# Matmuls without a reader at the norms of a two-layer Hyena and Mamba backbone

## The chip, the cores and the metric

The kernel runs on one core of one Trainium2 chip. The core has a matrix engine (TensorE, PE in the profile), a vector engine (VectorE, DVE), a scalar engine (ScalarE, ACT), a general engine (GpSimd, POOL) and a sync engine (SP) that issues most of the DMAs. The engines run their own instruction streams in order and meet at semaphores: an instruction can wait until a counter has reached a value, and can raise one when it is done. The metric is the device time of one execution in microseconds (us); less is better.

## The reference

Two layers over 256 latent tokens and 256 context tokens of width 1024. Every sub-layer is a norm with shift and scale, something in the middle, and a gated residual. What matters here is that each sub-layer begins with a root-mean-square over the whole width of a token, so nothing of the next product can start before the last piece of the residual stream is known:

```python
def rms_norm(x, eps=EPS):
    return x * lax.rsqrt(jnp.mean(x * x, axis=-1, keepdims=True) + eps)
def adaln(x, mod, k):
    return rms_norm(x) * (1 + mod[:, :, k + 1]) + mod[:, :, k]
def swiglu(h, w_in, w_out):
    g, u = jnp.split(h @ w_in, 2, axis=-1)
    return (jax.nn.silu(g) * u) @ w_out

h = h + 0.5 * mod[2] * swiglu(adaln(h, mod, 0), ffn_in[i, 0], ffn_out[i, 0])
a = adaln(h, mod, 3)                       # the mixer's input
y = hyena_mixer(a, ...)   # layer 0;  mamba2_mixer(a, ac, ...) in layer 1
h = h + mod[5] * y
h = h + 0.5 * mod[8] * swiglu(adaln(h, mod, 6), ffn_in[i, 1], ffn_out[i, 1])
```

The context stream does the same until the second mixer. The last line of the program is one more norm. Everything is float32.

## The kernel before, in words

The residual stream `hT` stays in SBUF as 8 tiles of 128 channels by 512 tokens (256 latent, 256 context; from the second mixer's output on only the 256 latent ones). A float32 product is done as three matmuls of a split operand pair (`mm3`, L1490): high by high, high by low, low by high. The high part of a weight chunk (`wh`, 128 x 2048) is made by ACT (`split_hi`, L553, work at L558), the low part (`wl`) by DVE (`split_lo`, L880, work at L883), both from `raw`, into which SP loads the weights. Each of the three is double-buffered. The semaphores are `w_hi`, `w_lo` (the chunk's low part is there, thus its high part too) and `w_used` (PE is done with a chunk). PSUM has eight banks of 512 columns; bank 7 belongs to the norms, and bank 0 to a chunk's first output tile.

The sub-layers have keys: "00" (FFN), "hy" (Hyena), "01" (FFN), "10" (FFN), "mb" (Mamba), "11" (FFN), "fin" (the last norm). A norm goes like this, with the engine ahead of each step:

1. DVE adds the last residual tile (L961; after the Hyena output L1193 and L1198), ACT squares it into `tt[1]` (L639), raising `sq_done`. The squares of the seven earlier tiles were added up into `acc` by POOL (L1430, `acc_done`).
2. PE sums over the channels: four matmuls with `acc` (L1502), then four with `tt[1]` (L1505), one for each 128 tokens, each one column wide (two of each for 256 tokens). The last raises `nsum`.
3. ACT takes the root (`root`, L575), DVE the reciprocal (L919, `rms_inv`).
4. PE spreads the result over the partitions with four transposes into bank 7 (L1515; two for 256 tokens), raising `rms_bc`.
5. For each of the 8 tiles k: DVE scales (`scaled`, L938), ACT makes the high part `xh` (L583), DVE the low part `xl` (`low`, L946), raising `p_lo`. DVE does them in the order scaled(0), scaled(1), low(0), scaled(2), low(1) and so on, then the low part of the second weight chunk (`second_lo`, L932). ACT makes the high part of that chunk ahead of its last tile.
6. PE starts the next sub-layer with `first_pair` (L1522): for every k it waits for `p_lo` and does the six matmuls of the first weight chunk, and then, after a wait for `w_lo` of the second chunk, the 48 matmuls of that one.

The low part of the first chunk of the next sub-layer is made before the last residual tile in four of the five norms in question ("hy", "10", "mb", "11"). In "01", which follows the Hyena output, ACT starts that split (L755) behind the last square and ahead of the root, and DVE its part (L1199) behind the last residual and ahead of the reciprocal.

The order on each engine is the order in which the code is written.

Of the kernel before, what the change touches and what calls it, by code (L numbers as in the profile page):

```python
# [11 lines left out]
P = 128  # L12
# [3 lines left out]
NT = 2 * L  # L16
# [114 lines left out]
def build(nc, t, out, kscr, afscr, cscr):  # L131
# [3 lines left out]
    ffn_in, ffn_out, norms = {}, {}, {}  # L135
# [18 lines left out]
    HYIN = Place(plan, w=12, zf=24)  # L154
# [7 lines left out]
    XB = Place(plan, w=12, conv=24)  # L162
# [8 lines left out]
    with ExitStack() as ctx:  # L171
        top = [16512]

        def at(name, shape, dt, offset):
            return nc.alloc_sbuf_tensor_at(name, shape, dt, offset=offset)
# [13 lines left out]
        def sem(name):  # L189
            return ctx.enter_context(nc.semaphore(name))  # L190
# [41 lines left out]
        wh = [at(f"wh{i}", [P, CW], F32R, o_w + i * 8 * KB) for i in range(2)]  # L232
# [55 lines left out]
        bank = [banks[i // 2][:, i % 2, :] for i in range(8)]  # L288
# [3 lines left out]
        w_lo = sem("w_lo")  # L292
# [1196 lines left out]
        def _(pe):  # L1489
            def mm3(dst, wslot, lo, x_hi, x_lo, start, stop):  # L1490

                h, l_ = wh[wslot][:, lo:lo + P], wl[wslot][:, lo:lo + P]
                pe.matmul(dst, h, x_hi, start=start, stop=False)  # L1493
                pe.matmul(dst, h, x_lo, start=False, stop=False)  # L1494
                return pe.matmul(dst, l_, x_hi, start=False, stop=stop)  # L1495

            def norm_sums(key, n=NT):
                pl = norms[key]
                cols = n // P
                pe.wait_ge(acc_done, pl.h - 1)  # L1500
                for j in range(cols):
                    pe.matmul(bank[7][:, j:j + 1], acc[:, j * P:j * P + P], ones[:, 0:1], start=j == 0, stop=False)  # L1502
                pe.wait_ge(sq_done, pl.h)
                for j in range(cols):
                    ins = pe.matmul(bank[7][:, j:j + 1], tt[1][:, j * P:j * P + P], ones[:, 0:1], start=False, stop=j == cols - 1)  # L1505
                    if j == cols - 2:
                        ins.then_inc(acc_done, 1)
                ins.then_inc(nsum, 1)

            def norm_spread(key, n=NT):  # L1510
                pl = norms[key]
                cols = n // P
                pe.wait_ge(rms_inv, pl.norm + 1)
                for j in range(cols):
                    ins = pe.transpose(bank[7][:, j * P:j * P + P], rs[:, j:j + 1].to_broadcast([P, P]), ident)  # L1515
                ins.then_inc(rms_bc, 1)

            def norm(key, n=NT):
                norm_sums(key, n)
                norm_spread(key, n)  # L1520

            def first_pair(pl, q, n=NT):  # L1522

                def tiles(u, k):
                    for s in range(2):
                        ins = mm3(bank[2 * u + s][:, 0:n], (pl.w + u) % 2, k * 256 + s * P, xh[:, k, 0:n], xl[:, k, 0:n],
                                  k == 0, k == DT - 1)
                    if k == DT - 1:
                        ins.then_inc(w_used, 1)
                pe.wait_ge(w_lo, pl.w + 1)  # L1530
                for k in range(DT):
                    pe.wait_ge(p_lo, q + k + 1)
                    tiles(0, k)
                pe.wait_ge(w_lo, pl.w + 2)
                for k in range(DT):
                    tiles(1, k)

            def two_tiles(wslot, banks, q, split=p_lo, n=NT):

                for k in range(DT):  # L1540
                    pe.wait_ge(split, q + k + 1)
                    for s in range(2):
                        ins = mm3(bank[banks + s][:, 0:n], wslot, k * 256 + s * P, xh[:, k, 0:n], xl[:, k, 0:n],
                                  k == 0, k == DT - 1)
                ins.then_inc(w_used, 1)

            def ffn(key, n=NT):

                if key != "00":
                    norm(key, n)  # L1550
                pi, po = ffn_in[key], ffn_out[key]
                x0 = norms[key].q
                def pair(i):
                    if i == 0:
                        pe.wait_ge(gate_ready, pi.gate)
                        first_pair(pi, x0, n)
                    for u in range(2 if i else 0):
                        pe.wait_ge(w_lo, i * 2 + (pi.w + u + 1))
                        if u == 0:
                            pe.wait_ge(gate_ready, i * 2 + pi.gate)  # L1560
                        else:
                            pe.wait_ge(p_ready, i * 2 + pi.q)
                        two_tiles((pi.w + u) % 2, 2 * u, x0, n=n)
                for i in range(FT // 2):
                    pair(i)

                def mpair(i, last):
                    for um in range(2):
                        pe.wait_ge(h_done, i * 2 + (po.h + um - 1))
                        for half in range(2):  # L1570
                            u = um * 2 + half
                            n_ = po.w + u
                            pe.wait_ge(w_lo, i * 4 + (n_ + 1))
                            if u == 0:
                                pe.wait_ge(p_lo, pi.q + FT - 2)
                            for kk in range(11):
                                k = half * 11 + kk
                                if k == FT - 2 and um == 0:
                                    pe.wait_ge(p_lo, pi.q + FT)
                                ins = mm3(bank[4 + um][:, 0:n], n_ % 2, kk * P, gh[:, k, 0:n], gl[:, k, 0:n],  # L1580
                                          k == 0, k == FT - 1)
                            ins.then_inc(w_used, 1)
                for i in range(DT // 2):
                    mpair(i, i == DT // 2 - 1)
# [75 lines left out]
            pe.wait_ge(mods_out, 1)  # L1660
            pe.wait_ge(s_set, 2)
            norm_sums("00")
            spectra(3, 2, 4)
            norm_spread("00")
            spectra(3, 4, 5)


            ffn("00")
            norm("hy")
            def hy_pair(i, last):  # L1670
                if i == 0:
                    pe.wait_ge(z_free, HYIN.zf)
                    first_pair(HYIN, norms["hy"].q)
                for u in range(2 if i else 0):
                    pe.wait_ge(w_lo, i * 2 + (HYIN.w + u + 1))
                    pe.wait_ge(z_free, i * 4 + (HYIN.zf + 2 * u - 2))
                    two_tiles((HYIN.w + u) % 2, 2 * u, norms["hy"].q)
# [66 lines left out]
            for j in range(4):  # L1744
# [5 lines left out]
                else:  # L1750
                    for s in range(2):
                        for k in range(DT):
                            ins = mm3(bank[2 + s][:], (HYOUT.w + 3) % 2, k * 256 + s * P, xh[:, k, :], xl[:, k, :],
                                      k == 0, k == DT - 1)
                        ins.then_inc(w_used if s else hy_half, 1)
            ffn("01")


            ffn("10")
            norm("mb")  # L1760
            x0 = norms["mb"].q

            def wide(pl, chunks, free, base, n):
# [223 lines left out]
```

## Time and profile before

| | us |
|---|---|
| three runs, median (lowest to highest) | 2147.05 (2145.24 to 2148.67) |
| the profiled execution, its own time | 2147.36 |
| its span, first to last instruction | 2145.5 |
| PE busy | 2001.8 (93%) |
| DVE busy | 1321.3 (62%) |
| ACT busy | 686.0 (32%) |
| POOL busy | 202.8 (9%) |

The mean granted TensorE clock over the span is 0.971 of full speed. In rows of the timeline the first number is the start of an instruction in us from the start of the span, the second how long it (or the run of alike instructions, "x4") took, and the bracket how long the engine had waited before it and for what.

### The profile page before, as it was taken

What the parts mean: (1) busy time and instruction counts of PE and PEld (TensorE: products, weight loads), DVE (VectorE), ACT (ScalarE), POOL (GpSimd) and SP (SyncE); (2) the same over time, 40 slices, a digit from 0 to 9 for tenths busy, and PEclk for the clock granted to TensorE, in tenths of its full rate; (3) what the DMA queues carried; (4) which work ended last, traced back from release to release, by engine and by line L of the source; (5) the groups of instructions that cost most, each with busy time, mean ns of one, the idle gap of its engine ahead of it and who ended that gap; (6) DMA issues with size and microseconds to landing.
All of it is one profiled execution on the core that took longest, in us unless ns stands there. A gap on an engine that the chain in (4) does not pass through costs nothing. (4 is left out here: it accounts for less than half of the span.)

```text
span 2145.5 us, 24954 instructions
## 1 busy us (share of the span) xinstructions
PE 2001.8 (93%) x10136; PEld 1672.0 (78%) x10136; DVE 1321.3 (62%) x1844; ACT 686.0 (32%) x913; POOL 202.8 (9%) x140
## 2 busy tenths in 40 slices
PE   5899999999989989999999999999899797698998
PEld 2688888878867868888887888888787784398998
DVE  6565546777857675554767565567765548845544
ACT  3422222232200232222224222222444335634442
POOL 1000000100023400000110000011000003340001
PEclk9999999999989999999999999999999898999999
DMA  8444435544520154442645444355432322444554
GB/s 322 152 159 155 137 106 183 165 139 135 179 76 1 41 165 148 139 155 83 201 153 171 138 152 143 104 173 165 147 118 89 118 84 74 123 133 152 186 155 141
DMA packets 274590, 298.25 MB, mean 139 GB/s; under 512 B 8912, under 2 KB 249136, under 8 KB 272688
## 3 DMA queue, kind: packets, MB, share of 16 engines
q1 hardware_dynamic: 270784, 285.44, 41.6%
q10 hardware_dynamic: 3696, 11.27, 1.4%
q8 instruction: 78, 1.28, 0.3%
q14 instruction: 32, 0.26, 0.0%
HBM read 290.31 MB, written 6.37 MB: 138 GB/s over the span
## 5 line engine op out<-in xcount | busy, mean ns | idle before, releaser
L1493 PE MATMUL banks<-xh,wh 128*128 128x512 f32 (+1 forms) x2120 | 782.3, 369 | 53.1 <-DVE xl L946 16.4
L1494 PE MATMUL banks<-xl,wh 128*128 128x512 f32 (+1 forms) x2120 | 777.0, 366 | 0.0
L1495 PE MATMUL banks<-xh,wl 128*128 128x512 f32 (+1 forms) x2120 | 776.4, 366 | 0.0
L883 DVE TENSOR_TENSOR wl<-raw,wh 128x2048 fp32r<-128x2048 f32 (+1 forms) x195 | 404.2, 2073 | 333.0 <-ACT wh L558 331.9
L558 ACT ACTIVATE wh<-raw 128x2048 fp32r<-128x2048 f32 (+1 forms) x201 | 349.6, 1739 | 644.6 <-PE banks L1495 562.9
L1493 PEld LDWEIGHTS banks<-xh,wh 128*128 128x128 f32 x2120 | 408.4, 193 | 124.5 <-issue 27.5
L1494 PEld LDWEIGHTS banks<-xl,wh 128*128 128x128 f32 x2120 | 408.4, 193 | 62.4
L1495 PEld LDWEIGHTS banks<-xh,wl 128*128 128x128 f32 x2120 | 407.8, 192 | 63.1
L1493 PE MATMUL banks<-gh,wh 128*128 128x512 f32 (+1 forms) x704 | 255.7, 363 | 2.9 <-DVE wl L883 1.6
L1494 PE MATMUL banks<-gl,wh 128*128 128x512 f32 (+1 forms) x704 | 255.2, 362 | 0.0
L1495 PE MATMUL banks<-gh,wl 128*128 128x512 f32 (+1 forms) x704 | 255.1, 362 | 0.0
L994 DVE TENSOR_TENSOR pp<-tt,banks 128x512 f32<-128x512 f32 (+1 forms) x88 | 50.7, 617 | 185.3 <-PE banks L1495 185.2
L1493 PEld LDWEIGHTS banks<-gh,wh 128*128 128x128 f32 x704 | 132.8, 189 | 24.5 <-DVE wl L883 2.2
L1494 PEld LDWEIGHTS banks<-gl,wh 128*128 128x128 f32 x704 | 132.8, 189 | 20.6
L1495 PEld LDWEIGHTS banks<-gh,wl 128*128 128x128 f32 x704 | 132.8, 189 | 20.4
L605 ACT ACTIVATE tt<-banks 128x512 f32<-128x512 f32 (+1 forms) x88 | 43.1, 542 | 271.0 <-PE banks L1495 271.0
L1430 POOL TENSOR_TENSOR acc<-acc,tt 128x512 f32<-128x512 f32 (+1 forms) x42 | 85.9, 2045 | 373.5 <-ACT tt L639 310.7
L1424 POOL MEMSET acc<- 128x512 f32 x6 | 3.2, 527 | 1176.0 <-DVE gl L974 931.4
L961 DVE SCALAR_TENSOR_TENSOR hT<-banks,mods,hT 128x256 f32<-128x256 f32 (+1 forms) x64 | 28.8, 481 | 108.2 <-PE banks L1495 108.2
L897 DVE SCALAR_TENSOR_TENSOR banks<-ada_rawo,cb 128x1024 f32<-128x1024 f32 x48 | 81.8, 1705 | 2.8 <-DMA ada_rawo<-in_ada_rest 2.8
L899 DVE SCALAR_TENSOR_TENSOR ada_rawf<-ada_rawf,cb 128x1024 f32<-128x1024 f32 x60 | 73.5, 1225 | 2.0
L897 DVE SCALAR_TENSOR_TENSOR banks<-ada_rawf,cb 128x1024 f32<-128x1024 f32 x60 | 73.7, 1228 | 0.0
(211 smaller groups left out, 1730.5 us busy)
## 6 DMA issues: line engine op xcount, KB each, us to landing
raw<-in_ffn_in SPq DMA_DIRECT2D x88, 1024.0 KB, 5.1
raw<-in_ffn_out SPq DMA_DIRECT2D x64, 704.0 KB, 4.8
ada_rawf<-in_ada_rest SPq DMA_DIRECT2D x60, 512.0 KB, 3.9
ada_rawo<-in_ada_rest SPq DMA_DIRECT2D x48, 512.0 KB, 4.0
raw<-in_mb_in_w SPq DMA_DIRECT2D x24, 1024.0 KB, 5.4
raw<-in_hy_in_w SPq DMA_DIRECT2D x12, 1024.0 KB, 5.2
afb<-decays SPq DMA_DIRECT2D x32, 256.0 KB, 3.1
raw<-in_mb_out_w SPq DMA_DIRECT2D x8, 1024.0 KB, 5.8
```

Source lines behind the costliest of these rows:

```text
L558: return act.activation(wh[n % 2][:, 0:cols], raw[r_slot][:, 0:cols], ACT.Copy).then_inc(w_hi, 1)
L605: act.activation(tt[u][:, 0:n], bank[u][:, 0:n], ACT.Silu).then_inc(gate_ready, 1)
L883: dve.tensor_tensor(wl[n_slot][:, 0:cols], raw[r_slot][:, 0:cols], wh[n_slot][:, 0:cols].bitcast(F32), ALU.subtract).then_inc(w_lo, 1)
L897: own(dve.scalar_tensor_tensor(banks[free][:].rearrange("p a n -> p (a n)"), pieces[i][:], half, cb0[:], ALU.mult, ALU.mult, accum_out=mod ...
L899: dve.scalar_tensor_tensor(pieces[i][:], pieces[i][:], half, c_ctx[:], ALU.mult, ALU.mult, accum_out=mods[layer][:, m, 1:2]).then_inc(ada_ ...
L961: ins = dve.scalar_tensor_tensor(x, bank[4 + um][:, w * L:w * L + L], mods[layer][:, i * 2 + (DT * k5 + um), w:w + 1], x, ALU.mult, ALU.add)
L994: dve.tensor_tensor(pp[(pi.q + u) % 2][:, 0:n], tt[u][:, 0:n], bank[2 + u][:, 0:n], ALU.mult).then_inc(p_ready, 1)
L1424: pool.memset(acc[:], 0.0).then_inc(acc_zero, 1)
L1430: pool.tensor_tensor(acc[:, 0:n], acc[:, 0:n], tt[um][:, 0:n], ALU.add).then_inc(acc_done, 1)
L1493: pe.matmul(dst, h, x_hi, start=start, stop=False)
L1494: pe.matmul(dst, h, x_lo, start=False, stop=False)
L1495: return pe.matmul(dst, l_, x_hi, start=False, stop=stop)
```

## The change

In five of the seven norms PE gets 19 additional matmuls, each 128 columns of `wh` of the coming chunk as the stationary operand by 512 columns of the same tile, into bank 0. Nothing reads the result: the first matmul of the next chunk begins bank 0 anew. Six stand between the sums over `acc` and the sums over the last square, two between the sums and the spread, eleven between the spread and the first chunk. Ahead of the six is a new wait for `w_lo` of the coming chunk, so that `wh` is known to be complete. The norms are "hy", "01", "10", "mb" and "11"; "00" and "fin" stay as they were. That is 5 x 19 = 95 matmuls.

```diff
+            def idle_turns(pl, count):
+                for _ in range(count):
+                    pe.matmul(bank[0][:], wh[pl.w % 2][:, 0:P], wh[pl.w % 2][:, 0:512], start=True, stop=True)
+
-            def norm_sums(key, n=NT):
+            def norm_sums(key, n=NT, nxt=None):
                 pl = norms[key]
                 cols = n // P
                 pe.wait_ge(acc_done, pl.h - 1)
                 for j in range(cols):
                     pe.matmul(bank[7][:, j:j + 1], acc[:, j * P:j * P + P], ones[:, 0:1], start=j == 0, stop=False)
+                if nxt:
+                    pe.wait_ge(w_lo, nxt.w + 1)
+                    idle_turns(nxt, 6)
                 pe.wait_ge(sq_done, pl.h)
...
-            def norm(key, n=NT):
-                norm_sums(key, n)
+            def norm(key, n=NT, nxt=None):
+                norm_sums(key, n, nxt)
+                if nxt:
+                    idle_turns(nxt, 2)
                 norm_spread(key, n)
+                if nxt:
+                    idle_turns(nxt, 11)
...
                 if key != "00":
-                    norm(key, n)
+                    norm(key, n, ffn_in[key])
...
-            norm("hy")
+            norm("hy", nxt=HYIN)
...
-            norm("mb")
+            norm("mb", nxt=XB)
```

Only PE's stream changes. At the norm "hy" it read before (`w_lo` and the other names in brackets are the semaphores waited for; `tt_114` is `tt[1]`, `wh_90` is `wh[0]`):

```order
L1502 MATMUL banks<-ones,acc 128x1 [waits acc_done]
L1502 MATMUL banks<-ones,acc 128x1 x3
L1505 MATMUL banks<-ones,tt_114 128x1 [waits sq_done]
L1505 MATMUL banks<-ones,tt_114 128x1 x3
L1515 MATMUL banks<-small,rs 128x128 [waits rms_inv]
L1515 MATMUL banks<-small,rs 128x128 x3
L1493 MATMUL banks<-xh,wh_90 128x512 [waits p_lo,w_lo,z_free]
```

and reads now (line numbers after the first added line are higher: L1506 is the old L1502, L1512 the old L1505, L1522 the old L1515, and L1499 is the added matmul):

```order
L1506 MATMUL banks<-ones,acc 128x1 [waits acc_done]
L1506 MATMUL banks<-ones,acc 128x1 x3
L1499 MATMUL banks<-wh_90 128x512 [waits w_lo]
L1499 MATMUL banks<-wh_90 128x512 x5
L1512 MATMUL banks<-ones,tt_114 128x1 [waits sq_done]
L1512 MATMUL banks<-ones,tt_114 128x1 x3
L1499 MATMUL banks<-wh_90 128x512 x2
L1522 MATMUL banks<-small,rs 128x128 [waits rms_inv]
L1522 MATMUL banks<-small,rs 128x128 x3
L1499 MATMUL banks<-wh_90 128x512 x11
L1493 MATMUL banks<-xh,wh_90 128x512 [waits p_lo,w_lo,z_free]
```

The sums over the last square now stand behind a wait for `w_lo` and six matmuls of 512 columns. At "01" and "10" the rows are the same but for `gate_ready` in place of `z_free`. At "11", the norm with 256 tokens, PE's stream was

```order
L1502 MATMUL banks<-ones,acc 128x1 [waits acc_done]
L1502 MATMUL banks<-ones,acc 128x1
L1505 MATMUL banks<-ones,tt_114 128x1 [waits sq_done]
L1505 MATMUL banks<-ones,tt_114 128x1
L1515 MATMUL banks<-small,rs 128x128 [waits rms_inv]
L1515 MATMUL banks<-small,rs 128x128
L1493 MATMUL banks<-xh,wh_91 128x256 [waits p_lo,w_lo,gate_ready]
```

and is now

```order
L1506 MATMUL banks<-ones,acc 128x1 [waits acc_done]
L1506 MATMUL banks<-ones,acc 128x1
L1499 MATMUL banks<-wh_91 128x512 [waits w_lo]
L1499 MATMUL banks<-wh_91 128x512 x5
L1512 MATMUL banks<-ones,tt_114 128x1 [waits sq_done]
L1512 MATMUL banks<-ones,tt_114 128x1
L1499 MATMUL banks<-wh_91 128x512 x2
L1522 MATMUL banks<-small,rs 128x128 [waits rms_inv]
L1522 MATMUL banks<-small,rs 128x128
L1499 MATMUL banks<-wh_91 128x512 x11
L1493 MATMUL banks<-xh,wh_91 128x256 [waits p_lo,w_lo,gate_ready]
```

The added matmuls keep their 512 columns here, while those of the sub-layer have 256.

## Rows read from the trace of the kernel before

**Rows 1.** Timeline, the norm "hy" from its sums to the first product
```profile
448.42 0.95 PE L1502 MATMUL banks<-ones,acc 128*128 128x1 f32 x8
449.53 0.63 ACT L639 ACTIVATE tt<-hT 128x512 f32<-128x512 f32 x1 [5.70 <-DVE hT L961]
450.21 1.05 PE L1505 MATMUL banks<-ones,tt 128*128 128x1 f32 x8 [0.84 <-ACT tt L639]
451.30 0.26 ACT L575 ACTIVATE rs<-banks,eps 128x4 f32<-128x4 f32 x1 [1.14 <-PE banks L1505]
...
451.83 0.75 PE L1515 MATMUL banks<-small,rs 128*128 128x128 f32 x4 [0.57 <-DVE rs L919]
452.62 1.66 DVE L938 SCALAR_TENSOR_TENSOR xt<-hT,mods,banks 128x256 f32<-128x256 f32 x4 [0.84 <-PE banks L1515]
...
455.49 0.77 PE L1493 MATMUL banks<-xh,wh 128*128 128x512 f32 x1 [2.91 <-DVE xl L946]
```

**Rows 2.** Windows, PE alone: start:end, length, busy (matmuls), PEclk, DMA share, GB/s
```profile
1000.00:1050.00 50.00, 50.00 (x223) 1.00 0.58 173
1950.00:2000.00 50.00, 50.00 (x419) 1.00 0.57 187
455.49:459.00 3.51, 3.51 (x8) 0.50 0.97 369
1939.31:1943.70 4.39, 4.39 (x20) 0.50 0.00 0
766.50:768.20 1.70, 0.00 (x0) 0.50 0.00 0
```

**Rows 3.** Timeline, the end of the first chunk of "hy" and the start of the second
```profile
466.01 0.88 DVE L946 SCALAR_TENSOR_TENSOR xl<-xt,mods,xh 128x256 fp32r<-128x256 f32 x2 [1.21 <-ACT xh L583]
466.81 2.28 DVE L932 TENSOR_TENSOR wl<-raw,wh 128x2048 fp32r<-128x2048 f32 x1
466.95 0.19 PEld L1493 LDWEIGHTS banks<-xh,wh 128*128 128x128 f32 x1 [0.38 <-DVE xl L946]
...
469.15 0.50 PE L1493 MATMUL banks<-xh,wh 128*128 128x512 f32 x1 [0.55 <-DVE wl L932]
```

**Rows 4.** Timeline, the spread of the norm "10" and what follows
```profile
1137.71 0.65 PE L1515 MATMUL banks<-small,rs 128*128 128x128 f32 x4 [0.57 <-DVE rs L919]
1138.40 1.66 DVE L938 SCALAR_TENSOR_TENSOR xt<-hT,mods,banks 128x256 f32<-128x256 f32 x4 [0.74 <-PE banks L1515]
```

**Rows 5.** Timeline, the norm "01" from the first chunk's high part to the scaling
```profile
763.95 1.89 ACT L558 ACTIVATE wh<-raw 128x2048 fp32r<-128x2048 f32 x1
764.09 1.05 PE L1505 MATMUL banks<-ones,tt 128*128 128x1 f32 x8 [1.69 <-ACT tt L639]
765.87 2.29 DVE L883 TENSOR_TENSOR wl<-raw,wh 128x2048 fp32r<-128x2048 f32 x1 [2.50 <-ACT wh L558]
768.08 0.17 DVE L919 RECIPROCAL rs<-rs 128x4 f32<-128x4 f32 x1
...
768.30 1.12 PE L1515 MATMUL banks<-small,rs 128*128 128x128 f32 x4 [3.16 <-DVE rs L919]
769.46 1.66 DVE L938 SCALAR_TENSOR_TENSOR xt<-hT,mods,banks 128x256 f32<-128x256 f32 x4 [1.21 <-PE banks L1515]
```

**Rows 6.** Timeline, the norm "11" with 256 tokens
```profile
1934.26 0.42 ACT L639 ACTIVATE tt<-hT 128x256 f32<-128x256 f32 x1 [2.45 <-DVE hT L961]
...
1934.47 1.02 PE L1502 MATMUL banks<-ones,acc 128*128 128x1 f32 x4 [3.11 <-POOL acc L1430]
...
1935.35 0.99 PE L1505 MATMUL banks<-ones,tt 128*128 128x1 f32 x4
...
1936.89 0.69 PE L1515 MATMUL banks<-small,rs 128*128 128x128 f32 x2 [0.55 <-DVE rs L919]
1937.62 0.87 DVE L938 SCALAR_TENSOR_TENSOR xt<-hT,mods,banks 128x256 f32<-128x256 f32 x2 [0.78 <-PE banks L1515]
...
1948.22 0.39 PE L1493 MATMUL banks<-xh,wh 128*128 128x256 f32 x1 [0.92 <-DVE wl L932]
```

## The prediction

> **What bounds the kernel now.** I read the page first: PE is busy 93% of the span, so what counts is the time in which it does nothing or runs at the lower clock. Then I read the granted clock in windows of 1 and 0.5 us around each norm, and the timeline of each norm. A norm is a serial chain, PE to ACT to DVE to PE to DVE, with PE mostly idle. At "hy" it goes: sums over `acc` done at 449.37, idle 0.84 until the square is there, sums from 450.21, root at 451.30, spread at 451.83, scaling at 452.62, first product at 455.49 [rows 1]. "10" and "mb" have the same pattern within 0.1 us.
>
> The clock falls to its lower level (1.2 of 2.4 GHz) in this quiet stretch: the first product of "hy" runs 8 matmuls in 3.51 us at a granted clock of 0.50, where PE at full clock does 223 in 50 us [rows 2]. That is 0.44 us against 0.224 us a matmul of 512 columns. (At half clock the steady step is 0.43: 0.427 by the starts in the timeline.) With 256 columns it is 0.22 against 50/419 = 0.119 [rows 2].
>
> Does the slow start cost anything? What the reader is to see is at the end of the first chunk. PE had caught up with DVE by the last tile: it waited 0.38 us for `xl` of the last k, and then again 0.55 us for the low part of the second chunk, which DVE started only when the last `xl` was done [rows 3]. From the scaling on, the pace is DVE's: the steps scaled and low take about 1.57 us for each k, where PE at full clock needs 6 x 0.226 = 1.36. All five norms end the first chunk with a wait of 0.5 to 0.9 us for L932; at "11" it is 0.92 [rows 6]. So in the trace the cold matmuls are hidden already, and the time at which the second chunk starts is set by `rms_bc`, that is by how soon the sums, the root and the spread are through. That short chain is what the change puts work into.
>
> **The change part by part.** An added matmul takes 0.226 us at full clock and 0.43 at half, and the first of a row some 0.11 to 0.14 more: in the timeline the second matmul behind a wait starts 0.34 (full) or 0.57 (half) after the first.
>
> *The six ahead of the last sums, "hy", "10", "mb".* They can start at about 449.30, when the sums over `acc` are issued, and take 0.11 + 6 x 0.226 = 1.47, to 450.77. The square is ready at 450.16 and its sums started at 450.21 [rows 1]. PE takes its matmuls in order, so these are late by 0.56. Bounds: 0.4 (the added row starts 0.15 sooner, under the tail of the sums) to 0.75 (the weights of the first are not loaded ahead). The spread gets a little shorter with the clock held: from its start to the scaling it is 0.79 at "hy", where the clock fell inside it, and 0.69 at "10", where it did not [rows 1, 4]; at "mb" it is 0.89. That gives back 0.1, 0 and 0.2. The wait for `w_lo` costs nothing: the low part was there at 446.2 in the timeline (L883 from 443.94, 2.29 us), ahead of the sums; without that cover it would cost as at "01". Sum of the three: 3 x 0.56 - 0.3 = 1.4; range 0.9 to 2.2.
>
> *The new wait, "01".* Here `wl` is made from 765.87 to 768.16, behind the last residual [rows 5]. Before, PE did its sums at 764.09, while ACT and DVE split the chunk, and only the reciprocal at 768.08 waited for that split. Now the sums themselves wait for it, with everything that hangs on them. PE gets through at 768.2 with the clock at 0.50 [rows 2]. Six added matmuls at half clock: 0.57 + 5 x 0.427 = 2.7, to 770.9. The sums took 0.99 for two groups of tokens at half clock [rows 6], so about 1.95 for the four of this norm, and 1.05 at full [rows 5]; root at 772.95 or 772.0. Root to spread is 0.53 [rows 1], and two cold matmuls (1.0) do not fit under it: 0.4 more. Spread to scaling takes 1.16 at half clock [rows 5], 0.69 at full [rows 4]. Scaling thus starts at 775.0 if the clock stays low, and at 773.25 if it is up by the sums, against 769.46: late by 5.5 or 3.8. I take 4.9, nearer the slow end: at "hy" the first 8 matmuls of 512 columns all ran at 0.50 [rows 2], and here only six stand ahead of the sums.
>
> *The six at "11".* `acc` is late here (PE waited 3.11 us for POOL), the clock is at 0.50, and the last square is ready at 1934.68, ahead of the end of the first sums: the second sums followed at 1935.35 without a gap [rows 6]. There is no idle time for the six to fill. They cost their full 2.7 us. The two behind the sums cost up to 0.45 if cold, nothing if the clock is up by then, and a faster spread gives back 0.2. I take 2.8; bounds 2.3 and 3.4.
>
> *The eleven behind the spread.* At full clock 0.11 + 11 x 0.226 = 2.6, against 2.9 of waiting for `xl` [rows 1]: they fit at "hy", "10", "mb". At half clock they take 4.8 and run over by 1.9 (3.1 at "11", where the wait is 1.7), but PE then does the chunk at full clock: 42 matmuls take 9.5 us, and DVE needs 466.89 - 455.35 = 11.5 to bring the last `xl`. Cost 0; bound 0.3 at "11", where 48 x 0.119 = 5.7 us of work would end just about when the second chunk is ready.
>
> *The clock in the first chunk.* The matmuls get faster, and PE waits longer for DVE instead. Gain 0; the other end is the rival below.
>
> Behind the first chunk PE is busy without a gap for tens of us [rows 2], SP's base and weight loads hang on `rms_bc` or on the splits, and all shift along. Nothing absorbs the delay.
>
> Sum: 1.4 + 4.9 + 2.8 = 9.1 us, bounds 7.0 and 11.1. The profiled execution took 2147.36, 0.3 above the median, so it stands for it: 2147.36 + 9.1 = 2156.5.
>
> **The rivals.**
>
> *The warm clock pays (the other side).* If the first chunk is paced by PE, its cold matmuls are a cost that goes away: 8, 9, 9 and 8 of 512 columns at four norms and 20 of 256 at "11", of which the first and the last are shown [rows 2], thus 34 x 0.2 + 20 x 0.1 = 8.8 us. Together with the delays 2147.7, no change; were the delays also smaller than I make them, faster, down to 2139. For it: a fall of the clock at all five norms, each with some 3.3 to 4.4 us at 0.50. Against it: the wait for the last `xl` [rows 3]. It decides from the point where PE comes to the last tile later than DVE; at "10" it was exactly level, at "11" 0.5 behind, and in both the wait for L932 was still there. The Trainium skill ("TensorE: Matmul & The Clock Gate", Why this matters for your kernels) advises to keep TensorE busy, since idle stretches between bursts send the clock to half; by it the sum would be near this rival's 2147.7. The trace agrees that the clock falls, and disagrees that here it costs.
>
> *The added matmuls make way.* If the six cost nothing at the sums, only the wait for `w_lo` at "01" is left: sums at 768.2, cold, root at 770.25, scaling at 771.95, late by 2.5: 2149.9. For it: only the idle 0.84 us at three norms. Against it: 1.47 is more than 0.84, and at "11" there is no idle time at all [rows 6]. The same page (The mechanism) has it that matmuls start and end in strict order; no row here shows a matmul that overtakes another.
>
> *The clock is not held.* The sums and the spread have columns of 1 and 128, and the clock may fall all the same. Then at "hy", "10", "mb" the two cost 0.4 and the spread is 0.4 longer, 2.4 in all, and "01" and "11" come at their slow ends, 0.6 more each: 2160.1.
>
> **How the numbers follow.** The forecast 0.72, with a range of its own of 2154.4 to 2158.5; the clock that pays 0.06; the matmuls that make way 0.10; the clock not held 0.12. About 0.2% (4.3 us) is what a measurement can tell from no change. The forecast and the third rival are slower by more: 0.84. The second rival (+2.5) and most of the first are within: 0.13. Faster is left with 0.03. The range takes in the third rival and a part of the way to the second: 2151.5 to 2160.5.
>
> **What the changed profile would show.** Right: at "hy" no idle time ahead of the sums over the square, which start 0.4 to 0.75 us after it is ready; at "01" PE idle until `wl` is done, and 6 us and more between the square and its sums; at "11" six matmuls of 0.43 us between the two rows of sums; PEclk 1.00 in the first chunks, with longer waits for `xl` in them than before, and the second chunk's start still bound to L932. From the end of the last residual to the second chunk each norm is longer by the terms above. Wrong: if that stretch is as long as before at "hy" or shorter, if PE's waits for `xl` and L932 vanish, or if the scaling at "01" begins within 3 us of where it did.

## The result and the profile after

| | before | changed |
|---|---|---|
| median of 7 runs, us (lowest to highest) | 2147.05 (2141.39 to 2148.76) | 2155.68 (2152.27 to 2158.01) |
| span of the profiled execution, us | 2145.5 | 2153.3 |
| PE busy, us | 2001.8 | 2022.3 |
| mean granted clock | 0.971 | 0.977 |

The changed kernel is slower: ratio 1.0046, 95% interval 1.0033 to 1.0059. The forecast was 2156.5. PE is busier by 20.5 us and its clock higher on the mean, and neither tells how the time changed: the 95 matmuls that nobody reads take 29.7 us of the busy time, and the first chunks, now at full clock, take less of it than before.

The norm "hy" in the timeline of the changed kernel (start, duration, engine, line; the rows answer to [rows 1]; rows of weight loads, PEld, are left out here and below):

```profile
448.73 0.94 PE L1506 MATMUL banks<-ones,acc 128*128 128x1 f32 x8
448.93 0.88 DVE L961 SCALAR_TENSOR_TENSOR hT<-banks,mods,hT 128x256 f32<-128x256 f32 x2 [2.40 <-PE banks L1495]
449.54 1.65 PE L1499 MATMUL banks<-wh 128*128 128x512 f32 x6
449.84 0.63 ACT L639 ACTIVATE tt<-hT 128x512 f32<-128x512 f32 x1 [5.71 <-DVE hT L961]
451.02 0.95 PE L1512 MATMUL banks<-ones,tt 128*128 128x1 f32 x8
451.83 0.71 PE L1499 MATMUL banks<-wh 128*128 128x512 f32 x2
452.01 0.26 ACT L575 ACTIVATE rs<-banks,eps 128x4 f32<-128x4 f32 x1 [1.53 <-PE banks L1512]
...
452.54 0.65 PE L1522 MATMUL banks<-small,rs 128*128 128x128 f32 x4
452.94 2.77 PE L1499 MATMUL banks<-wh 128*128 128x512 f32 x11
453.23 1.66 DVE L938 SCALAR_TENSOR_TENSOR xt<-hT,mods,banks 128x256 f32<-128x256 f32 x4 [0.74 <-PE banks L1522]
...
456.10 0.47 PE L1493 MATMUL banks<-xh,wh 128*128 128x512 f32 x1 [0.39 <-DVE xl L946]
```

The square is ready at 450.47, and its sums start at 451.02: the bracket with the wait for the square is gone, because PE is now the late one. Compare the bracket of 0.84 before [rows 1]. From the start of these sums to the scaling it is 2.21 us instead of 2.41. Half of the 0.20 is the spread, 0.65 us instead of 0.75, with the clock held. The other half is the sums, 0.95 instead of 1.05, and this is not the clock, which was full in both: they now follow other matmuls without idle time. Net 0.30 later. The first product waits 0.39 for `xl` instead of 2.91, which sounds like a gain and is none: the eleven only fill the time.

The end of the first chunk (to be laid beside [rows 3]):

```profile
466.62 0.88 DVE L946 SCALAR_TENSOR_TENSOR xl<-xt,mods,xh 128x256 fp32r<-128x256 f32 x2 [1.21 <-ACT xh L583]
467.42 2.28 DVE L932 TENSOR_TENSOR wl<-raw,wh 128x2048 fp32r<-128x2048 f32 x1
467.56 0.50 PE L1493 MATMUL banks<-xh,wh 128*128 128x512 f32 x1 [0.42 <-DVE xl L946]
...
469.76 0.50 PE L1493 MATMUL banks<-xh,wh 128*128 128x512 f32 x1 [0.55 <-DVE wl L932]
```

From the scaling (453.23) to the second chunk (469.76) it is 16.53 us. Before it was 469.15 - 452.62 = 16.53.

The norm "01" (beside [rows 5]):

```profile
761.27 0.69 DVE L1198 TENSOR_TENSOR hT<-hT,tt 128x512 f32<-128x512 f32 x1
761.99 0.63 ACT L639 ACTIVATE tt<-hT 128x512 f32<-128x512 f32 x1 [4.80 <-DVE hT L1198]
762.53 1.89 ACT L558 ACTIVATE wh<-raw 128x2048 fp32r<-128x2048 f32 x1
764.45 2.29 DVE L883 TENSOR_TENSOR wl<-raw,wh 128x2048 fp32r<-128x2048 f32 x1 [2.50 <-ACT wh L558]
766.80 2.93 PE L1499 MATMUL banks<-wh 128*128 128x512 f32 x6 [5.82 <-DVE wl L883]
769.53 1.70 PE L1512 MATMUL banks<-ones,tt 128*128 128x1 f32 x8
771.09 1.20 PE L1499 MATMUL banks<-wh 128*128 128x512 f32 x2
...
772.09 1.05 PE L1522 MATMUL banks<-small,rs 128*128 128x128 f32 x4
772.79 3.82 PE L1499 MATMUL banks<-wh 128*128 128x512 f32 x11
773.18 1.65 DVE L938 SCALAR_TENSOR_TENSOR xt<-hT,mods,banks 128x256 f32<-128x256 f32 x4 [1.44 <-PE banks L1522]
```

The new wait shows as a bracket of 5.82 us for L883 where 1.69 for the square stood. The sums start 6.91 us after the square is ready, not 0.05. The six run at half clock, and so do the sums (1.70) and the spread (1.05): the granted clock over each of the three is 0.50.

The norm "11" (beside [rows 6]):

```profile
1938.40 0.61 PE L1506 MATMUL banks<-ones,acc 128*128 128x1 f32 x4 [3.09 <-POOL acc L1430]
1938.87 2.81 PE L1499 MATMUL banks<-wh 128*128 128x512 f32 x6
1941.47 0.85 PE L1512 MATMUL banks<-ones,tt 128*128 128x1 f32 x4
...
1942.87 0.43 PE L1522 MATMUL banks<-small,rs 128*128 128x128 f32 x2
1943.06 2.75 PE L1499 MATMUL banks<-wh 128*128 128x512 f32 x11
1943.34 0.87 DVE L938 SCALAR_TENSOR_TENSOR xt<-hT,mods,banks 128x256 f32<-128x256 f32 x2 [0.53 <-PE banks L1522]
```

The square (ready at 1938.61) waits 2.86 us for PE. The six (2.60 from start to start) and the last sums ran at a granted clock of 0.50, the sums over `acc` and the spread at full clock.

Divided at the start of the scaling, the five norms give the account. "Ahead" is from the end of the last residual tile (L961, at "01" L1198) to the first L938, "behind" from there to the first matmul of the second chunk, both read from row starts:

| norm | ahead, before | ahead, changed | behind, before | behind, changed | forecast | measured |
|---|---|---|---|---|---|---|
| hy | 3.12 | 3.42 | 16.53 | 16.53 | +0.46 | +0.30 |
| 01 | 6.09 | 11.22 | 16.53 | 16.53 | +4.9 | +5.13 |
| 10 | 3.02 | 3.42 | 16.53 | 16.53 | +0.56 | +0.40 |
| mb | 3.22 | 3.42 | 16.53 | 16.53 | +0.36 | +0.20 |
| 11 | 3.39 | 5.18 | 10.60 | 10.60 | +2.8 | +1.79 |

The sum is 7.8 us, and the spans differ by 2153.3 - 2145.5 = 7.8. That the two agree so well is in part luck. The change touches nothing outside the norms, and yet two stretches there differ between the two profiles: from the second chunk of "hy" to the last residual of "01" the changed kernel is 2.0 us shorter, and from the second chunk of "11" to the end it is 2.0 us longer. Such differences come and go between executions. Take the five stretches from the last residual to the third chunk out of the spans of all twelve profiles of this document, and what is left lies between 1994.3 us (e4_early) and 1999.8 (e6_fit). So a single span cannot confirm a term of 1 or 2 us, but the stretches of the norms can, as long as they repeat themselves; below it is said where they do not.

The clock in the first chunks of the changed kernel, in windows as in [rows 2], the first at "hy", the second at "01":

```profile
456.00:459.50 3.50, 3.40 (x13) 1.00 0.96 368
776.50:780.00 3.50, 3.50 (x17) 1.00 1.03 359
```

The clock is where the change wants it: over the first 3 us of the first chunk it is 1.00 at all five norms, where it was 0.50 at all five before. The stretch "behind" did not get shorter by 0.01 us.

### The profile page after: what moved, and what is told of

It is laid out like the page before. It is cut to its first block and busy times, and to the rows that moved or that the text cites. A ratio compares the mean times of both kernels' runs of the same rounds, so it can differ in the third digit from the quotient of the medians.

```text
span 2153.3 us, 25144 instructions
## 1 busy us (share of the span) xinstructions
PE 2022.3 (94%) x10231; PEld 1681.8 (78%) x10231; DVE 1321.3 (61%) x1844; ACT 686.9 (32%) x913; POOL 202.8 (9%) x140
## 3 DMA queue, kind: packets, MB, share of 16 engines
q8 instruction: 79, 1.29, 0.3%
## 5 line engine op out<-in xcount | busy, mean ns | idle before, releaser
L883 DVE TENSOR_TENSOR wl<-raw,wh 128x2048 fp32r<-128x2048 f32 (+1 forms) x195 | 404.2, 2073 | 341.6 <-ACT wh L558 340.5
L961 DVE SCALAR_TENSOR_TENSOR hT<-banks,mods,hT 128x256 f32<-128x256 f32 (+1 forms) x64 | 28.7, 480 | 102.3 <-PE banks L1495 102.3
```

The source lines that it names most:

```text
L883: dve.tensor_tensor(wl[n_slot][:, 0:cols], raw[r_slot][:, 0:cols], wh[n_slot][:, 0:cols].bitcast(F32), ALU.subtract).then_inc(w_lo, 1)
L961: ins = dve.scalar_tensor_tensor(x, bank[4 + um][:, w * L:w * L + L], mods[layer][:, i * 2 + (DT * k5 + um), w:w + 1], x, ALU.mult, ALU.add)
```

## The experiments

The theory to be tested is the chain: what counts is the time up to the scaling; behind it DVE paces both engines. The main rival is the warm clock: the matmuls at half clock do cost, and the loss hides the return of that cost.

**The eleven alone** (e1_eleven), edited from the changed kernel.

```diff
-                if nxt:
-                    pe.wait_ge(w_lo, nxt.w + 1)
-                    idle_turns(nxt, 6)
...
-                if nxt:
-                    idle_turns(nxt, 2)
```

> Only the eleven matmuls behind the spread are kept, at all five norms; the six, the two and the wait for w_lo are gone. Chain theory (only what stands ahead of the scaling counts, and DVE sets the pace of the first chunk): no change, 2147 within 1.5 us; from the end of the last residual to the second chunk each norm is as long as before (19.6, 22.6, 19.6, 19.7, 14.0 us), although the eleven may run at half clock and end later than the first xl. Warm-clock theory (the cold matmuls of the first chunk cost time, and the change's loss hides their return): faster by up to 8.8 us, about 2139.

Measured: 2147.45 against 2145.72 of the kernel before, measured beside it; ratio 1.0008 (0.9997 to 1.0019), not told from no change, and far from the 2139 of the rival. Ahead: 3.02, 6.09, 3.03, 3.32, 3.39; behind: 16.53 four times and 10.60. At "11":

```profile
1935.08 0.69 PE L1519 MATMUL banks<-small,rs 128*128 128x128 f32 x2 [0.55 <-DVE rs L919]
1935.42 4.20 PE L1499 MATMUL banks<-wh 128*128 128x512 f32 x11
1939.46 0.28 PE L1493 MATMUL banks<-xh,wh 128*128 128x256 f32 x1
...
1946.41 0.39 PE L1493 MATMUL banks<-xh,wh 128*128 128x256 f32 x1 [1.04 <-DVE wl L932]
```

The eleven ran mostly at half clock and held the first product back to 3.65 us behind the scaling (1935.81), where it came 1.69 behind it before [rows 6]. Still PE waited 1.04 us for L932 at the end. In this run too the clock is at 1.00 over the first 3 us of all five first chunks. So these eleven are free, neither cost nor gain, and the warm clock in the first chunk does not pay in this program with its order as it is. The first rival is out.

**Without "01"** (e2_not01).

```diff
-                    norm(key, n, ffn_in[key])
+                    norm(key, n, ffn_in[key] if key != "01" else None)
```

> The whole change, but not at the norm 01. Chain theory: the stretches of the changed kernel, in which 01 was 5.1 us longer than before and the other four together 2.7, say 2147.3 + 2.7 = 2150. Theory that the 95 matmuls cost by their number (8 us over 95): 76/95 of the loss, 2153.5. Warm-clock theory: no statement.

Measured: 2148.83 against 2145.72 of the kernel before, ratio 1.0014 (1.0004 to 1.0024). That is +3.1 (0.9 to 5.1 by the interval), beside 2.7 by the chain and 6.2 by number. "01" is back at 6.08 ahead. One norm of five carries two thirds of the loss. The stretches ahead of the scaling add up to 2.3 here, and at "11" there is a loss that they do not show: the clock fell at the start of the second chunk (0.51 from 1951.00 to 1954.40, against 1.00 before), and that chunk took 7.36 us instead of 5.85. PE is busy for all of these 3.4 us: there it is the bound, and a low clock costs.

**The wait alone** (e3_wait01).

```diff
+                if key == "01":
+                    pe.wait_ge(w_lo, ffn_in["01"].w + 1)
                 pe.wait_ge(sq_done, pl.h)
```

> The kernel before with only the wait for w_lo ahead of the last sums at 01, no matmul added. Chain theory: sums at 768.2 instead of 764.1 at half clock (1.95 us), root, reciprocal, cold spread: the scaling is late by 2.5 us, 2149.6. Rival (the wait is covered, since the reciprocal waits for the same low part anyway): no change, 2147.

Measured: ratio 1.0009 (0.9999 to 1.0019). The interval has no change at its edge, so the time alone decides nothing. The timeline does:

```profile
764.99 2.29 DVE L883 TENSOR_TENSOR wl<-raw,wh 128x2048 fp32r<-128x2048 f32 x1 [2.50 <-ACT wh L558]
767.34 1.87 PE L1507 MATMUL banks<-ones,tt 128*128 128x1 f32 x8 [5.82 <-DVE wl L883]
769.24 0.26 ACT L575 ACTIVATE rs<-banks,eps 128x4 f32<-128x4 f32 x1 [4.28 <-PE banks L1507]
769.54 0.18 DVE L919 RECIPROCAL rs<-rs 128x4 f32<-128x4 f32 x1 [2.25 <-ACT rs L575]
769.77 1.11 PE L1517 MATMUL banks<-small,rs 128*128 128x128 f32 x4 [0.57 <-DVE rs L919]
```

Sums at half clock (1.87 for the eight passes), then root, reciprocal, spread, one behind the other. Ahead at "01" is 8.43 instead of 6.09: the wait costs 2.34 us (2.5 expected). The edit does not touch "11", and yet "11" has 2.59 ahead in this profile instead of 3.39, with the sums over `acc` at full clock (0.61 us instead of 1.02). This norm differs by 0.8 between executions by itself. The remaining 2.8 of the 5.13 are the added matmuls. It is the two waits in series that cost: before, the sums and the split ran side by side and only the reciprocal saw the later of the two.

**Twelve for six** (e8_twelve), in e2_not01.

```diff
-                    idle_turns(nxt, 6)
+                    idle_turns(nxt, 12)
```

> The changed kernel without 01 (as e2_not01), with twelve matmuls in place of the six ahead of the last sums. Chain theory: each added matmul there delays the scaling by 0.226 us at full clock: hy, 10 and mb 1.36 longer each than with six (last residual to scaling 4.8 instead of 3.4), 11 by 1.4 to 2.6; in all 5.5 to 6.7 us over e2_not01, 2154.5 to 2156. The scaling to the second chunk stays at 16.53 and 10.60.

Measured, in four runs: 2155.95, ratio 1.0049 (1.0033 to 1.0064). Ahead: 4.79, 4.80, 4.80 at "hy", "10", "mb", which is 1.38 more for six more matmuls, 0.23 each. At "11" 7.78 instead of 4.83, 2.95 more, above the 2.6 I had allowed; 0.4 of it is the sums over `acc`, at half clock here (1.01 us) and at full in e2_not01 (0.61). Behind: 16.53 or 16.54, and 10.60. At "hy":

```profile
448.61 3.03 PE L1499 MATMUL banks<-wh 128*128 128x512 f32 x12
448.91 0.63 ACT L639 ACTIVATE tt<-hT 128x512 f32<-128x512 f32 x1 [5.68 <-DVE hT L961]
451.47 0.95 PE L1512 MATMUL banks<-ones,tt 128*128 128x1 f32 x8
```

At these three norms the loss goes with the matmuls queued ahead of the sums, one for one.

**Only where they fit** (e6_fit), in the kernel before. The four numbers are the added matmuls ahead of the sums over `acc`, ahead of the last sums, behind the sums and behind the spread; each such row stands behind a wait for `w_hi` of the coming chunk. The function that issues them and its four calls are left out here.

```diff
+            FIT = {"hy": (0, 3, 2, 11), "10": (0, 3, 2, 11), "mb": (0, 3, 2, 11), "01": (0, 0, 9, 11), "11": (11, 0, 2, 6)}
```

> The kernel before with added matmuls only where PE's wait is longer than they are: three (not six) ahead of the last sums at hy, 10, mb, two behind the sums; at 01 none ahead of the sums and nine behind them, once the chunk's high part is there; at 11 eleven ahead of the sums over acc (in the 3.1 us of waiting for POOL), two behind the sums; eleven (six at 11) behind the spread. Chain theory: nothing is delayed, the clock is held through the short chain: the end of the last residual to the scaling gets shorter by 0.1 (hy), 0 (10), 0.1 to 0.3 (mb), 0.4 to 0.5 (01) and about 1.2 (11), the stretch from the scaling to the second chunk stays at 16.53 and 10.60; 1.9 us less than before, 2144 to 2145.5. Warm-clock theory: about 8 us more than that, 2137.

Measured: 2147.93 against 2146.68, ratio 1.0008 (0.9999 to 1.0017): the gain of 1.9 that was expected is not there. Three of the five norms came out as expected ahead of the scaling and two did not: "hy" 3.02 (-0.10), "mb" 3.03 (-0.19), "11" 2.33 (-1.06, though "mb" and "11" came to 3.02 and 2.59 in e3_wait01 without an added matmul), but "01" 6.91 (+0.82) and "10" 3.49 (+0.47). At "11" the second chunk took the gain back: the clock was at 0.57 in its first 3.4 us, and it took 7.15 us instead of 5.85. At "01":

```profile
765.99 3.87 PE L1505 MATMUL banks<-wh 128*128 128x512 f32 x9 [0.75 <-ACT wh L558]
768.18 0.17 DVE L919 RECIPROCAL rs<-rs 128x4 f32<-128x4 f32 x1
769.66 0.68 PE L1527 MATMUL banks<-small,rs 128*128 128x128 f32 x4
```

and the clock there, in windows (PE busy, PEclk):

```profile
766.00:767.00 1.00, 1.00 (x3) 0.71 0.00 0
767.00:769.50 2.50, 2.50 (x7) 0.50 0.00 0
```

I had reckoned nine at full clock (2.15 us). The clock fell all the same while they ran, they took 3.87, and the reciprocal, ready at 768.35, waited 1.3 for PE. At "10" five added matmuls ahead did not keep the clock from falling inside the spread, which took 1.12 us. So a filler that fits only at full clock may not fit. Behind is 16.53 or 16.54 again, and 10.60 at "11".

**The second chunk earlier** (e4_early). If DVE's order is the bound behind the scaling, that order is what should be changed. ACT makes its half of the second chunk sooner as well, and PE does two steps of that chunk between those of the first, so the edit changes the order of all three engines, not of DVE alone. No matmul is added:

```diff
@@ ACT, norm_hi @@
+                if key != "00":
+                    next_hi(w, 0, 0, 2)
                 for k in range(DT):
...
-                    if k == DT - 2:
-                        if key == "00":
-                            act.wait_ge(k_used, DT)
+                    if k == DT - 2 and key == "00":
+                        act.wait_ge(k_used, DT)
                         next_hi(w, 0, 0, 2)
@@ DVE, norm @@
                     low(k)
-                second_lo()
+                    if k == 1 and key != "00":
+                        second_lo()
+                if key == "00":
+                    second_lo()
@@ PE, first_pair @@
+                ahead = {2: 0, 4: 1} if pl.w else {}
                 for k in range(DT):
+                    if k in ahead:
+                        pe.wait_ge(w_lo, pl.w + 2)
+                        tiles(1, ahead[k])
                     pe.wait_ge(p_lo, q + k + 1)
                     tiles(0, k)
                 pe.wait_ge(w_lo, pl.w + 2)
-                for k in range(DT):
+                for k in range(len(ahead), DT):
                     tiles(1, k)
```

> No matmul added. At the five norms the second chunk's high part is made by ACT right behind the root, its low part by DVE behind the second low, and PE does two of the eight steps of the second chunk between the steps of the first. If DVE's order is what sets the time from the scaling on: the first two chunks end 1 to 1.5 us sooner at 01, 10 and 11, less at hy and mb where DVE has the taps behind them; 2142 to 2144. If PE at half clock is the bound there: no gain, 2147, or slower since the first chunk is finished 2 us later and the third chunk's split waits for it.

Measured: 2141.61 against 2145.72, ratio 0.9985 (0.9975 to 0.9995): faster. From the last residual to the third chunk (the 97th product matmul): "hy" 30.11 (31.17 before), "01" 32.79 (33.65), "10" 29.98 (30.59), "mb" 31.47 (32.69), "11" 19.71 (19.84); 3.9 us in all. The gain at "01" and "10" is less than the 1 to 1.5 expected, at "11" (0.13) next to nothing, and at "hy" and "mb" more; 0.2 of the 1.2 at "mb" stand ahead of the scaling, where the edit does nothing. DVE's low parts run on at their pace around the moved split:

```profile
455.72 0.88 DVE L947 SCALAR_TENSOR_TENSOR xl<-xt,mods,xh 128x256 fp32r<-128x256 f32 x2
456.51 2.28 DVE L933 TENSOR_TENSOR wl<-raw,wh 128x2048 fp32r<-128x2048 f32 x1
458.71 0.86 DVE L939 SCALAR_TENSOR_TENSOR xt<-hT,mods,banks 128x256 f32<-128x256 f32 x2
...
466.86 0.88 DVE L947 SCALAR_TENSOR_TENSOR xl<-xt,mods,xh 128x256 fp32r<-128x256 f32 x2 [0.19 <-ACT xh L585]
```

DVE's wait of 1.21 us for ACT at the last tile [rows 3] has shrunk to 0.19.

**Both** (e7_both), e4_early with the added matmuls of e6_fit.

> The matmuls of e6_fit in the kernel e4_early (second chunk prepared behind the second low, two of its steps between the steps of the first). There PE has no idle time left in the first two chunks of 01, 10 and 11, so a matmul at half clock is no longer hidden. Chain theory: besides the 1.9 us of e6_fit some 0.8 us for each of 01, 10 and 11 (1.8 us of slow matmuls, less the idle time that is left), thus 3 to 5 us under e4_early: 2137 to 2139. If the clock does not matter there either: only 1.9 us, 2140.

Measured: 2142.54, ratio 0.9983 (0.9974 to 0.9992), no better than e4_early, where 3 to 5 us had been expected. The two parts can be told apart in the timeline. From the scaling to the third chunk "01" takes 26.14 instead of 26.70 in e4_early, "10" 26.17 instead of 26.96 and "11" 16.06 instead of 16.32; "hy" and "mb" take as long as there. (Against the second profile of e4_early, e11_early_again below, it is 1.1, 1.1 and 0.2 less.) In e4_early PE does not wait once from the first product of "01" (768.71) to its third chunk, and the first 3.5 us of that run at 0.50; in e7_both the clock is at 1.00, and PE waits again for L933 (0.54 us). So where PE has work enough, the higher clock is worth 0.2 to 1.1 us at three of the norms. Ahead of the scaling "11" gains 1.06, "10" nothing (3.03), and "01" is 0.84 late, as in e6_fit, which takes back most of its gain or more. From the last residual to the third chunk the five norms take 1.9 us less than in e4_early. Why the median does not show them stays open.

**Fewer of them, and "11" alone** (e9_early_fit, e10_early_only11, with e4_early again as e11_early_again on the same chip).

```diff
-            FIT = {"hy": (0, 3, 2, 11), "10": (0, 3, 2, 11), "mb": (0, 3, 2, 11), "01": (0, 0, 9, 11), "11": (11, 0, 2, 6)}
+            FIT = {"hy": (0, 3, 2, 9), "10": (0, 3, 2, 9), "mb": (0, 3, 2, 9), "01": (0, 0, 5, 9), "11": (11, 0, 2, 6)}
... (e10_early_only11)
+            FIT = {"11": (11, 0, 2, 6)}
```

> e7_both with fewer added matmuls, five instead of nine between the sums and the spread at 01 (they would fit into the 2.3 us before the reciprocal even at half clock) and nine instead of eleven behind the spread. Chain theory: 01 no longer late (last residual to scaling 5.6 to 6.1 instead of 6.9), the rest as e7_both: 1 us under e7_both, and 1.5 to 3 under e4_early in the same call: 2139 to 2141. If the matmuls ahead of the scaling give nothing: level with e4_early.

> e4_early with added matmuls at the norm 11 alone (eleven ahead of the sums over acc, two behind the sums, six behind the spread). Chain theory: the stretch from the last residual of 11 to its third chunk is 1.3 us shorter than in e4_early (1.06 of it ahead of the scaling), nothing else moves: 1.3 us under e4_early.

> e4_early once more, on the chip of the two above, for a comparison of medians: 0.9985 of the kernel before, by both theories.

| | median, us | ratio to the kernel before | 95% interval |
|---|---|---|---|
| e9_early_fit | 2138.42 | 0.9971 | 0.9962 to 0.9980 |
| e10_early_only11 | 2140.12 | 0.9976 | 0.9968 to 0.9985 |
| e11_early_again | 2140.79 | 0.9977 | 0.9967 to 0.9986 |
| kernel before, same chip | 2145.10 | | |

e9_early_fit beats both kernels of the change and is 2.4 us under e11_early_again by the medians. The two intervals against the kernel before overlap, but its eleven times laid directly beside the twelve of e11_early_again give 2.2 us by the means, with an interval of 0.9 to 3.4. Its five matmuls at "01" took 2.50 us at half clock and were out of the way when the reciprocal was done (765.41): the spread followed at 765.46, and ahead of the scaling "01" is back at 6.09:

```profile
763.05 2.50 PE L1509 MATMUL banks<-wh 128*128 128x512 f32 x5
765.24 0.17 DVE L920 RECIPROCAL rs<-rs 128x4 f32<-128x4 f32 x1
765.46 1.11 PE L1531 MATMUL banks<-small,rs 128*128 128x128 f32 x4
```

From the last residual to the third chunk it takes 32.25 at "01" (33.35 in e11_early_again), 29.66 at "10" (30.28) and 18.39 at "11" (19.68). The 1.00 at "mb" (31.47 against 32.47) is not the added matmuls: e4_early has 31.47 too. The 1.29 at "11" are in e10_early_only11 too (18.39), as expected, and 1.06 of them stand ahead of the scaling (2.33 there in all four kernels with the eleven ahead of the sums; of the five profiles in which "11" has no added matmul ahead of the scaling, four have 3.39 and one 2.59); its median is only 0.7 lower, less than medians can tell.

## Why the prediction was right

The direction, the place and the order of the terms held; two sizes were off.

- *PE first idle, then paced by DVE* was right and carries the result. All seven kernels that leave the order of the engines alone, with the clock at either level in the first chunk, needed 16.53 or 16.54 us from the scaling to the second chunk. e4_early, which changes that order, got to the third chunk sooner. DVE is not alone in this stretch, which the prediction passes over: at its last tile DVE waits 1.21 us for ACT [rows 3], which makes the high part of the second chunk first. How much of the gain of e4_early is that wait, and how much PE's own new order, no run separates.
- *The six at "hy", "10", "mb"*, forecast 1.4 in all, came to 0.90 (0.30, 0.40, 0.20). The delay of the sums was nearly as worked out (0.55 between square and sums, 0.50 more than before, against 0.56). The spread gave back 0.1, 0 and 0.2 with the held clock, as credited. What the sum left out is the sums themselves, 0.1 shorter at each of the three since they follow other matmuls without a gap. e8_twelve gives the price of one such matmul directly: 0.23 us.
- *The new wait at "01"*, forecast 4.9 between 3.8 and 5.5, came to 5.13. e3_wait01 splits it: 2.34 for the wait (2.5), 2.8 for the matmuls. The clock stayed low through the sums and the spread, as in the slow case, and the sums were shorter than forecast (1.70 for 1.95).
- *The six at "11"*, forecast 2.8 with 2.3 as the lower bound, came to 1.79, below the bound. This is the mis-sized term. The six themselves took 2.60 (2.7 forecast). But I took the clock at 0.50 from the trace of before for the sums over `acc` as well, and in the changed kernel these ran at full clock: the row behind them starts 0.47 us after they do instead of 0.88, which is 0.41 less. From the last sums to the scaling it is 1.87 instead of 2.27, another 0.40: 0.26 from the spread, at full clock (0.43 for 0.69), and the rest from the last sums, still at half clock, but without idle time ahead of them (0.85 for 0.99). The first 0.41 come ahead of any added matmul, so they are luck of the execution and no work of the change: e3_wait01, in which "11" is as before, has them too, and 2.59 us ahead in all. Laid beside that 2.59 the term would be 2.6; in e2_not01 it was 1.44 beside 3.39. A bound that rests on the state of the clock in one execution is no bound.
- *The eleven* cost 0, as worked out, also when they ran at half clock (e1_eleven).
- *The rival that the warm clock pays* is refuted by e1_eleven for this program, and shown in part for another: in e4_early, where PE has less idle time in the first two chunks, the higher clock is worth 0.2 to 1.1 us at three of the five norms (e7_both). The advice of the Trainium skill to keep TensorE busy ("TensorE: Matmul & The Clock Gate", Why this matters for your kernels) thus paid here where PE was the bound, and not ahead of it.
- *The added matmuls make way* is refuted by e8_twelve, in which twelve delay as twelve.
- *The clock not held* happened in part: at "01" the sums and the spread were at the lower level (0.50), at "hy", "10", "mb" it held.

The total was 9.1 forecast, 7.8 by the spans and 8.6 by the medians of seven runs (7.1 to 12.7 by the interval). The medians come this close to the forecast in part by luck: by the stretches, "01" is 0.2 above its term, and the other four norms are 1.5 below theirs.

## What to carry to other kernels

Work put into an engine's idle time is free only if it ends before the thing waited for arrives, and that has to be reckoned at the lower clock, for every semaphore it waits on, and for what stands behind it in the same queue. A slow clock in a stretch costs nothing while another engine sets the pace: look at the last tile of the stretch, and whether PE waits there, before trying to raise it. Here it paid to change the order that made PE wait, and then to keep the clock up with few enough matmuls; the same few without the new order were not tried. And a fall of the clock that is avoided in one stretch can come in a later one, where it costs, as in the second chunk of "11" in e2_not01 and e6_fit.

## What was not expected of the hardware

The granted clock fell while PE was working. At "01" of e6_fit nine matmuls of 512 columns ran without a gap, after 0.75 us of waiting and eight short passes; the clock was at 1.00 in their first 0.4 us and at 0.50 from 767.00 on. At "10" it was at 0.50 over the spread, behind five added matmuls of 512 columns; the same five held it at "hy" and "mb", and at "10" in e7_both. And the same kernel can differ between two executions: e4_early had 3.02 us ahead of the scaling at "mb" in one profile and 4.02 in the other (e11_early_again), where the window over the sums and the spread shows

```profile
1501.00:1505.00 4.00, 2.71 (x12) 0.63 0.00 0
```

What decides it I did not settle. What these rows show is that a few matmuls put into a wait of one or two us held the clock in some executions and not in others.
